# A 512-token transformer stack on one core: causal mask of the sparse attention taken from the matmuls into VectorE's maximum, norm factors spread in f32r, and a few side operations in other places

## The reference

```python
def rmsnorm(x, g): x * rsqrt(mean(x*x)) * g          # seven of them
h = rmsnorm(x, norm); proj = h @ w                   # 128-wide strips of w
# layer 0: y = conv3(u * b) * c  (three-tap causal convolution), plus memory attention
# layer 1: sliding window attention with sinks, plus memory attention
# both:    x = x + (silu(h @ w_gate) * (h @ w_up)) @ w_down
# second block, sparse attention: 4 query blocks of 128, 8 heads in 2 groups
s = einsum('qghd,qgnbd->qghnb', q, ks) * scale       # selected keys: with 512 tokens all of them
p_s = masked_softmax(s, kpos <= t)                   # causal
p_w = masked_softmax(q @ kw * scale, causal window)  # window 512: again causal over all
p_c = masked_softmax(q @ kc, cmp_end <= t)           # 31 compressed keys
o = g0 * (p_c @ vc) + g1 * (p_s @ vs) + g2 * (p_w @ vw)
# retention over 4 heads; out = x + rmsnorm(merged @ w_out)
```

## Time and profile before

| | us |
|---|---|
| median of 3 runs | 1632.66 (1632.55 to 1633.41) |
| the profiled execution, its own time | 1633.12 |
| span of its trace | 1631.0 |
| TensorE busy | 1618.7 (99%) |
| VectorE busy | 876.8 (54%) |
| ScalarE busy | 573.2 (35%) |
| GpSimd busy | 124.7 (8%) |
| granted TensorE clock | 0.999 |

### The profile page before, as it was taken

How to read it: one execution, slowest core, us unless ns; L and a number is a source line. 1 busy time by engine, 2 the same in 40 slices (tenths; PEclk the granted TensorE clock), 3 DMA queues, 4 the chain that set the end, 5 groups by cost and what they waited for, 6 DMA issues and landing times.

```text
span 1631.0 us, 20597 instructions
## 1 busy us (share of the span) xinstructions
PE 1618.7 (99%) x7722; PEld 1300.9 (80%) x7722; DVE 876.8 (54%) x1190; ACT 573.2 (35%) x973; POOL 124.7 (8%) x114
## 2 busy tenths in 40 slices
PE   9999999999999999999999999999999999999998
PEld 7977888888888876778888888887777678888887
DVE  7566644444523366764444443337576656556444
ACT  6333432223222345543232223322345542234222
POOL 2000200000000000030000001114111001000000
PEclk9999999999999999999999999999999999999999
DMA  6422332322332341132322232243111121232222
GB/s 217 142 78 80 102 98 90 103 92 101 115 106 89 72 109 46 39 111 90 103 90 99 94 121 90 99 169 118 52 65 52 40 71 39 84 104 91 94 101 90
DMA packets 44588, 152.74 MB, mean 94 GB/s; under 512 B 5515, under 2 KB 8812, under 8 KB 44012
## 3 DMA queue, kind: packets, MB, share of 16 engines
q1 hardware_dynamic: 43744, 149.22, 27.9%
q10 hardware_dynamic: 780, 2.65, 0.6%
HBM read 149.46 MB, written 2.39 MB: 93 GB/s over the span
## 4 chain that ended last, share of the span: by engine, by line
PE 96%; DVE 2%; issue 1%; ACT 1%; DMA 0%; POOL 0%; DVEq 0%; POOLq 0%; ACTq 0%
PE ps L1841 27%; PE ps L1843 27%; PE ps L1842 27%; PE ps L2218 1%; PE ps L2232 1%; PE ps L2254 1%; PE ps L2278 1%; PE ps L2334 1%; PE ps L2333 1%; PE ps L2332 1%; PE ps L2042 1%; DVE w_lo L1109 1%; PE ps L2060 1%; PE ps L2075 1%; PE ps L2268 1%
## 5 line engine op out<-in xcount | busy, mean ns | idle before, releaser
L1841 PE MATMUL ps<-a_hi,w_hi 128*128 128x512 f32 x1336 | 530.6, 397 | 1.9 <-DVE a_lo L1114 1.1
L1843 PE MATMUL ps<-a_hi,w_lo 128*128 128x512 f32 x1336 | 520.8, 390 | 0.0
L1842 PE MATMUL ps<-a_lo,w_hi 128*128 128x512 f32 x1336 | 520.4, 390 | 0.0
L1109 DVE TENSOR_TENSOR w_lo<-raw,w_hi 128x1024 fp32r<-128x1024 f32 (+4 forms) x257 | 331.2, 1289 | 247.1 <-ACT w_hi L704 241.9
L704 ACT ACTIVATE w_hi<-raw 128x1024 fp32r<-128x1024 f32 (+4 forms) x257 | 270.2, 1051 | 284.1 <-PE ps L1843 264.5
L1841 PEld LDWEIGHTS ps<-a_hi,w_hi 128*128 128x128 f32 x1336 | 250.9, 188 | 62.6 <-issue 9.1
L1843 PEld LDWEIGHTS ps<-a_hi,w_lo 128*128 128x128 f32 x1336 | 250.8, 188 | 53.1
L1842 PEld LDWEIGHTS ps<-a_lo,w_hi 128*128 128x128 f32 x1336 | 251.1, 188 | 50.3 <-issue 1.0
L1135 DVE TENSOR_TENSOR tmp<-ps,rstd 128x512 f32<-128x512 f32 x121 | 83.5, 691 | 185.8 <-PE ps L1843 175.6
L1841 PE MATMUL ps<-g_hi,w_hi 128*128 128x512 f32 x352 | 136.9, 389 | 0.0
L1842 PE MATMUL ps<-g_lo,w_hi 128*128 128x512 f32 x352 | 136.9, 389 | 0.0
(11 more groups left out here) (301 smaller groups left out, 1811.5 us busy)
## 6 DMA issues: line engine op xcount, KB each, us to landing
raw<-w SPq DMA_DIRECT2D x134, 512.0 KB, 3.4
raw<-w8b SPq DMA_DIRECT2D x70, 512.0 KB, 3.4
raw<-w_down SPq DMA_DIRECT2D x32, 704.0 KB, 4.0
w<-cmp_w SPq DMA_DIRECT2D x2, 2048.0 KB, 10.7
raw<-w_out_first SPq DMA_DIRECT2D x8, 320.0 KB, 2.8
raw<-w_nsa_o SPq DMA_DIRECT2D x8, 256.0 KB, 2.8
out<-o_t SPq DMA_DIRECT2D x8, 256.0 KB, 2.0
x<-xT SPq DMA_DIRECT2D x7, 256.0 KB, 6.7
```

The costliest lines, as they stand in the source:

```text
L1109: dve.tensor_tensor(w_lo[:, slot, 0:w], raw[:, raw_slot, 0:w], w_hi[:, slot, 0:w].bitcast(F32), ALU.subtract).then_inc(w_lo_ready, 1)
L1841: pe.matmul(o, wh, a_h, start=start and at == 0, stop=False)
L1842: pe.matmul(o, wh, a_l, start=False, stop=False)
L1843: ins = pe.matmul(o, wl, a_h, start=False, stop=stop and at == kt - 1)
```

## The change

1. **Mask.** The four mask matmuls of each unit go. VectorE's one reduce becomes four `tensor_tensor_reduce` (one for each head), which read the scores from PSUM and a bf16 table `ahead` [128, 512], write the masked, negated scores to `p_n` and the bias to `nmx`. ScalarE's exponential then reads `p_n` in SBUF. The score banks are free after the maximum (`ns_max`) and no longer after the exponential. `ahead` is a new load of SP, behind `cmp_pe`; `masks` shrinks.
2. **Spreads.** `rs` is split into `rs_hi` and `rs_lo` by two small VectorE operations, two diagonals are made, and `spread` is two f32r matmuls. `diag_lo` lies over `acc`, so that GpSimd's `clear` waits for the spread before it.
3. **Places.** `spread(V_MIX0)` goes from tile 3 to 5 of strip 3, `spread(V_MEM)` from the border into tile 3 of strip 9, `spread(V_MIX1)` from tile 1 to 3. Four of the memory's eight squares go one and two strips later. The convolution of tile 0 goes from n=4 to n=5, behind `split(6)`. In N_OUT2 the squares come three strips later, VectorE's `operand` one strip later, and `split(N_FFN1+1)` behind the last operands. `sw_turn(7, 0)`, `hidden` and `ns_turn(15, (2, 3))` go from a border into the strip behind it. `ns_maxima` comes ahead of the `split` in VectorE's queue, ScalarE's `ns_normalise(0)` ahead of the compressed exponential, and `cmp_normalise` is cut in two.

The core of the diff:

```diff
             def clear(v):
                 if v:
-                    pool.wait_ge(norm_sum, v)
+                    pool.wait_ge(norm_spread, v)
...
-                if n in (3, 4):
-                    for k in range(4 * n - 12, 4 * n - 8):
+                if n in (3, 4, 5):
+                    for k in ((0, 1, 2, 3), (4, 5), (6, 7))[n - 3]:
                         square(V_MEM, k, k % 2, memx[:, k, :], NMEM, first=k < 2)
...
-            out_phase(N_OUT2, V_FFN1, G_FFN1)
+            for m in range(KT):
+                split(N_OUT2 + m + 2, late_width(N_OUT2 + m + 2))
+                act.wait_ge(lin_read, out_index(N_OUT2 + m) + 1)
+                operand(m, G_FFN1)
+                if m >= 3:
+                    square(V_FFN1, m - 3, (m - 3) % 2, x[:, m - 3, :], first=m < 5)
+            for k in range(KT - 3, KT):
+                square(V_FFN1, k, k % 2, x[:, k, :], first=False)
...
             def ns_exps(u):
-                b, jp, br, keys = ns_unit(u)
-                act.wait_ge(ns_max, u + 1)
-                if u >= 2:
-                    act.wait_ge(ns_turned, GH * (u - 1))
+                keys = ns_unit(u)[3]
                 for j in range(GH):
-                    act.activation(p_n[:, u % 2, j, 0:keys], ps[:, 2 + j, 0:keys], ACT.Exp,
-                                   bias=nmx[:, u % 2, j:j + 1], accum_out=den[:, u % 2, j:j + 1])\
+                    act.wait_ge(ns_max, GH * u + j + 1)
+                    act.activation(p_n[:, u % 2, j, 0:keys], p_n[:, u % 2, j, 0:keys], ACT.Exp,
+                                   bias=nmx[:, u % 2, j:j + 1], scale=-1.0, accum_out=den[:, u % 2, j:j + 1])\
                         .then_inc(ns_exp, 1)
...
             def diagonal(v, tiles=TB, rs=rs):
 
                 dve.wait_ge(norm_pow, v + 1)
-                dve.tensor_tensor(diag[:, 0:tiles, :],
-                                  ident[:].unsqueeze(1).to_broadcast([P, tiles, P]),
-                                  rs[:, 0:tiles].unsqueeze(2).to_broadcast([P, tiles, P]), ALU.mult)\
-                    .then_inc(norm_diag, 1)
+                if v:
+                    dve.wait_ge(norm_spread, v)
+                dve.tensor_copy(rs_hi[:, 0:tiles], rs[:, 0:tiles]).then_inc(norm_part, 1)
+                dve.wait_ge(norm_part, 2 * v + 1)
+                dve.tensor_tensor(rs_lo[:, 0:tiles], rs[:, 0:tiles], rs_hi[:, 0:tiles].bitcast(F32), ALU.subtract)\
+                    .then_inc(norm_part, 1)
+                dve.wait_ge(norm_part, 2 * v + 2)
+                for part, diag in ((rs_hi, diag_hi), (rs_lo, diag_lo)):
+                    dve.tensor_tensor(diag[:, 0:tiles, :],
+                                      ident[:].unsqueeze(1).to_broadcast([P, tiles, P]),
+                                      part[:, 0:tiles].bitcast(F32).unsqueeze(2).to_broadcast([P, tiles, P]),
+                                      ALU.mult).then_inc(norm_diag, 1)
...
                 elif what == 1:
                     scaled(n, bank, v_s[:])
...
+                    if i:
+                        convolve(n, i)
...
                 if n in (3, 4, 5, 9):
                     split(n + 1, KT * P)
+                if n == 5:
+                    convolve(N_CONV0 + 1, 0)
...
             for m in range(KT):
                 residual(m, N_OUT2 + m, out_bank(N_OUT2 + m))
-                split(N_OUT2 + m + 2, late_width(N_OUT2 + m + 2))
-                if m > 1:
-                    operand(m - 2, G_FFN1, 3 * KT + m - 1)
-            for k in (KT - 2, KT - 1):
+                if m < KT - 1:
+                    split(N_OUT2 + m + 2, late_width(N_OUT2 + m + 2))
+                if m > 2:
+                    operand(m - 3, G_FFN1, 3 * KT + m - 2)
+            for k in range(KT - 3, KT):
                 operand(k, G_FFN1, 3 * KT + k + 1)
+            split(N_FFN1 + 1, late_width(N_FFN1 + 1))
...
             def ns_maxima(u):
...
-                dve.tensor_reduce(nmx[:, u % 2, :], ps[:, 2:6, 0:keys], AX.X, ALU.max, negate=True)\
-                    .then_inc(ns_max, 1)
...
+                for j in range(GH):
+                    dve.tensor_tensor_reduce(p_n[:, u % 2, j, 0:keys], ps[:, 2 + j, 0:keys],
+                                             ahead[:, S - keys:S], -1.0, FAR, ALU.add, ALU.min,
+                                             nmx[:, u % 2, j:j + 1]).then_inc(ns_max, 1)
...
+                if NS_FIRST < n < NS_FIRST + NS:
+                    ns_maxima(n - NS_FIRST)
+                if n == NS_FIRST + 1:
+                    cmp_weights()
                 if n + 1 == N_GATE:
                     gate_split()
...
             def spread(v, tiles=TB):
 
-                pe.wait_ge(norm_diag, v + 1)
-                pe.matmul(ps[:, stat_bank, 0:tiles * P], ones[:],
-                          diag[:, 0:tiles, :].rearrange("p b t -> p (b t)"),
-                          start=True, stop=True).then_inc(norm_spread, 1)
+                pe.wait_ge(ones_r_ready, 1)
+                for part, diag in enumerate((diag_hi, diag_lo)):
+                    pe.wait_ge(norm_diag, 2 * v + part + 1)
+                    ins = pe.matmul(ps[:, stat_bank, 0:tiles * P], ones_r[:],
+                                    diag[:, 0:tiles, :].rearrange("p b t -> p (b t)"),
+                                    start=part == 0, stop=part == 1)
+                ins.then_inc(norm_spread, 1)
...
-                if n == 3 and at == 3:
+                if n == 3 and at == 5:
                     spread(V_MIX0)
+                if n == 9 and at == 3:
+                    spread(V_MEM, 2)
...
-                for k in range(GH):
-                    ins = pe.matmul(ps[:, 2 + k, b * P:keys], ident_b, causal, start=False, stop=True)
                 ins.then_inc(ns_scores, 1)
...
+                if k == 0 and u == NS - 1:
+                    ns_turn(u, (2, 3))
                 if k == 0 and ns_unit(u)[2]:
                     cmp_turn(u)
```

More of the change, by code:

```diff
@@ L96 @@
 EMPTY = -1.0e29
+FAR = 3.0e38
 TINY = float(np.finfo(np.float32).tiny)
@@ L135, in build @@
     diag_at = main[0]
-    diag = sb(main, "diag", [P, TB, P])
+    diag_hi = sb(main, "diag_hi", [P, TB, P], R32)
+    acc_at = main[0]
     acc = sb(main, "acc", [P, S])
@@ L141, in build @@
     acc2 = sb(main, "acc2", [P, S])
-    main[0] += K1
+    ahead = sb(main, "ahead", [P, S], BF16)
+    ones_r = sb(main, "ones_r", [P, P], R32)
     w2 = sb(main, "w2", [P, 2, 2, HD])
     ident = sb(main, "ident", [P, P])
-    masks = sb(main, "masks", [P, 2 * P + TB * NCMP], BF16)
+    masks = sb(main, "masks", [P, P + TB * NCMP], BF16)
     vc = sb(main, "vc", [NCMP, 2, HD])
@@ L155, in build @@
     kc = sb(rest, "kc", [P, 2 * NCMP])
+    rs_hi = sb(rest, "rs_hi", [P, TB], R32)
+    rs_lo = sb(rest, "rs_lo", [P, TB], R32)
     rs2 = sb(rest, "rs2", [P, TB])
@@ L250, in build @@
     ident_b = masks[:, 0:P]
-    causal = masks[:, P:2 * P]
-    mask_c = masks[:, 2 * P:].rearrange("p (b c) -> p b c", b=TB)
+    mask_c = masks[:, P:].rearrange("p (b c) -> p b c", b=TB)
     ps = nc.alloc_psum_tensor("ps", [P, 8, S], F32)
@@ L280, in build @@
     norm_diag = sem("norm_diag")
+    norm_part = sem("norm_part")
+    ones_r_ready = sem("ones_r_ready")
     norm_spread = sem("norm_spread")
@@ L370, in build @@
     ns_scores = sem("ns_scores")
+    ahead_in = sem("ahead_in")
     ns_max = sem("ns_max")
@@ L542, in _ @@
             sp.dma_start(pe2[:], a["cmp_pe"]).then_inc(small2_in, 16)
+            sp.dma_start(ahead[:], a["ahead"]).then_inc(ahead_in, 16)
             with sp.Fori(1, N_DOWN0 // RAW, 1) as i:
@@ L630, in power @@
                     .then_inc(norm_pow, 1)
+            pool.wait_ge(ones_ready, 1)
+            pool.tensor_copy(ones_r[:], ones[:]).then_inc(ones_r_ready, 1)
             clear(V_MIX0)
@@ L1219, in conv_low, with convolve @@
                     .then_inc(yc_lo_ready, 1)
+            def convolve(n, i):
+                dve.wait_ge(lin_read, n + 1)
+                dve.tensor_tensor(v_s[:], v_s[:], u_s[:], ALU.mult).then_inc(conv_step, 1)
+                dve.wait_ge(conv_step, 5 * i + 1)
+                dve.tensor_scalar(y_s[:], v_s[:], conv_w[:, i, 2:3], None, ALU.mult).then_inc(conv_step, 1)
+                for back in (1, 2):
+                    dve.wait_ge(conv_step, 5 * i + 1 + back)
+                    dve.scalar_tensor_tensor(y_s[:, back:S], v_s[:, 0:S - back],
+                                             conv_w[:, i, 2 - back:3 - back], y_s[:, back:S],
+                                             ALU.mult, ALU.add).then_inc(conv_step, 1)
             def l0_epilogue(n):
@@ L1953, in _ @@
                     sums(V_MEM, 2)
-                if n == 9:
-                    spread(V_MEM, 2)
                 if N_MEMKV + 6 <= n <= N_MEMKV + 9:
@@ L1977, in _ @@
                     else:
-                        strip(n, mem_hi, mem_lo, bank_of(n), cols=NMEM)
+                        strip(n, mem_hi, mem_lo, bank_of(n), cols=NMEM, aside=lambda at, n=n: begin_beside(n, at))
```

(29 more changed lines are left out.)

25 lines of the change are left out of this document (15 added, 10 removed).

## The result

The changed kernel takes 1635.95 us (median of 20 runs, 1633.47 to 1636.55), the kernel before 1632.79 (20 runs, 1632.19 to 1633.58). The ratio is 1.0017, 95% interval 1.0011 to 1.0024: 0.17% slower, less than the 0.2% that counts as a difference here, where 1628.2 us and "faster" had been forecast. The profiled execution took 1634.9 us with a span of 1633.1, against 1633.12 and 1631.0 before.

What follows compares the result with a forecast made beforehand. TensorE bounds the kernel, holding 96% of the chain of waits. Savings of 8.5 us (3.7 + 2.3 + 2.5) less costs of 4.05 (0.45 + 2.8 + 0.8) net 4.4 us: 1628.2 us median, range 1624.2 to 1631.5.

Steps and rivals of the forecast that it cites:

- No rival: Four rivals: convolution costs nothing 12%, FFN1 starts without waits 11%, maximum at half rate 5%, change does less 20%.
- Masks: In the 16 units: dropping four mask matmuls saves 0.23 us each, 3.7 us; VectorE's added work is hidden.
- waits of units 0 and 1: TensorE's waits in the first two units: 1.3 us by starts, 0.6 stays, so 0.7 us less.
- Rival (c): In the units: the new maximum runs at half rate for its bf16 operand, 15 us more, 1643 us; chance 5%.
- Spreads: Norm-factor spreads: two f32r matmuls instead of one plain; five save 2.05 us, the memory's 0.25, sum 2.3 us.
- wait on the low diagonal ahead of strip 187: Ahead of strip 187: nothing covers VectorE's longer chain, 0.45 us given back (bounds 0.3 and 0.7).
- Waits that go: TensorE waits at the memory's diagonal, sliding-window turn, `hidden` and the first two units go: 2.5 us less.
- Diagonal, window, `hidden`: Three TensorE waits that go: memory's diagonal 0.6 us by starts, sliding-window turn 0.5, `hidden` on the windows 0.7.
- `ns_turn(15, (2, 3))`: In the last unit: its 0.5 us wait only changes its name, gain taken as 0 (bounds 0 and 0.5).
- The convolution: Short strips: tile 0's convolution behind `split(6)` makes strip 7 wait for `w_lo`, 2.8 us more (bounds 2.3 and 3.5).
- Start of FFN1: Ahead of FFN1's second strip: sums wait for four late GpSimd sums, 0 to 1.9 us later, taken as +0.8.
- The signs given: No L2221, spreads at half distance, waits on `w_lo`, `acc` and low diagonal, none on L1585 in units 2 to 15.

Runs made afterwards that it cites:

- both moves undone: Changed kernel with tile 0's convolution back in strip 3's epilogue and the last projection's squares, operands and splits in their old order: 1626.06 us.
- the 13 added matmuls: Changed kernel with matmuls nobody reads in TensorE's long waits, 9 ahead of strip 7 and 13 ahead of FFN1's sums: 1632.09 us.
- best: Changed kernel with convolution and last projection back in their old order, except the split for FFN1's second strip stays behind the last operands: 1625.61 us.
- squares or order: Changed kernel with the convolution and ScalarE's last-projection squares back in their old places, VectorE's new order kept: 1625.27 us.

## Why the prediction was wrong

The forecast was 1628.2 us, the median 1635.95: 7.75 us more, outside the range of 1624.2 to 1631.5, and of the other sign. No rival held the outcome either. The steps, in the order of the prediction:

**Masks: right.** No L2221; no wait on VectorE's normalisation but 0.2 us in one unit. About 2.7 us by the two traces (3.4 over all units, less the 0.7 of the waits of units 0 and 1), 3.4 by the runs, for 3.7. Rival (c) fell: the new maximum runs at full rate, 0.69 us at 512 columns, which is the 0.7 estimated.
```profile
L1609 DVE CUSTOM_DVE_ANT_0 p_n<-ps,ahead 128x512 f32<-128x512 f32 x16 | 10.1, 688 | 6.4 <-PE ps L2267 6.4
```

**Spreads: right.** Between the two traces each spread gained its 0.4 us. Two f32r matmuls, 0.45 us from the first to the next tile:
```profile
743.38 0.39 PE L1922 MATMUL ps<-diag_hi,ones_r 128*128 128x512 f32 x1
743.60 0.39 PE L1922 MATMUL ps<-diag_lo,ones_r 128*128 128x512 f32 x1
743.83 0.39 PE L1884 MATMUL ps<-a_hi,w_hi 128*128 128x512 f32 x1
...
1110.83 0.19 PEld L1922 LDWEIGHTS ps<-diag_lo,ones_r 128*128 128x128 f32 x1 [0.35 <-DVE diag_lo L1149]
```
The last row is the wait on the low diagonal ahead of strip 187, 0.35 us by the record for 0.45 forecast. By the runs they are worth 1.2 us for the 1.85 forecast, and the difference is in the short strips, where the start-up also moves TensorE by more than that.

**Waits that go: right.** Diagonal, window, `hidden` and units 0 and 1 gained about what was written; `ns_turn(15, (2, 3))` gained nothing, the wait only changed its name (L2289 on L997, 0.6 us). The kernel with both moves undone gains 6.8 us in all, where these three parts were 3.7 + 2.3 - 0.45 + 2.5 = 8.05. By its starts 3.4 us of the gain are there at unit 0's scores (1154.92 against 1158.28 us), for the 3.65 forecast up to that point, and 3.3 come in the units, for 4.4: most of the 1.25 us short is in the units.

**The convolution: right in its wait, and the wait was only two thirds of its price.** The list has 2.9 us, for 2.8 (bounds 2.3 and 3.5); by starts it is 3.0, of which 1.3 only take back TensorE's lead from the start-up. What failed is that I stopped at the wait. Behind it the clock was at 1.2 GHz for 3.4 us, 1.5 us more in the profiled execution.

**Start of FFN1: the term that was mis-sized.** I took +0.8 us and up to 1.9. TensorE went from 0.9 us behind to 4.1 at the sums, 3.2 net. Two steps failed. I took the four sums left at 1.38 each, 5.5 us; they took 7.07, as VectorE's four operands and its split ran in the same time:
```profile
725.43 0.67 DVE L1171 TENSOR_TENSOR x<-x,ps 128x512 f32<-128x512 f32 x1
726.03 3.76 DVE L1129 SCALAR_TENSOR_TENSOR a_lo<-x,gains,a_hi 128x512 fp32r<-128x512 f32 x4
...
727.47 7.07 POOL L631 TENSOR_TENSOR acc<-acc,sq 128x512 f32<-128x512 f32 x4 [2.51 <-ACT sq L724]
729.72 2.30 DVE L1124 TENSOR_TENSOR w_lo<-raw,w_hi 128x1024 fp32r<-128x1024 f32 x1
```
That is 1.55 us. My own rows had half of it: a sum beside VectorE was 1.58 in the earlier trace rows, four of them are 6.3 us, and I took 1.38, near the 1.30 of one alone. And they began 0.4 us later against TensorE than written. The rest of the miss is that I settled on 0.8 where my sum gave 1.2. Then came the clock, 2.4 us more by starts, which I had not priced at all.

**The clock: the missing term.** Filling both waits gives 4.35 us back, over half of the 7.75. The prediction has no term for the clock, and so counts it as 1.00 throughout; it never asked what waits of three to four times the longest in the trace (1.0 us) would do to it. By the Trainium skill (TensorE: Matmul & The Clock Gate, Part 1: The HAM clock gate) the lower level is the default and activity lifts it. The runs here agree: the same two places with TensorE busy in them, 1.00 and 4.35 us less. With that page in mind the slower outcome could have stood as a rival. No run here shows when a wait is followed by a fall: behind the same 2.9 us one profile has it and one has not.

Together, from the medians: 4.35 us for the clock; 1.9 for the two moves without it (5.5 for 2.8 + 0.8), by the traces the start of FFN1 alone is 2.4 too much (3.2 for 0.8), and the convolution's move comes out somewhat below its 2.8; and 1.25 for what the rest gained less (6.8 for 8.05). These are 7.5 of the 7.75 us.

**The signs given** were there, L2221 gone, spreads at half the distance, 2.9 us on `w_lo` at strip 7, `acc` named by TensorE (until 734.6 us, not 731), but for 0.2 us on VectorE's normalisation in one late unit. They would have told me that the mechanisms were right, and none of them asks how long the price runs on behind a wait.

## What to carry to other kernels

Price a new long wait of TensorE with the stretch behind it: here waits of 2.0 to 3.8 us were followed by 1.2 GHz for 3.4 us or more in all profiled executions but one, and matmuls that nobody needs, put into the wait, won that part back. When work is shifted later, count what is left of it behind the last operand on the slowest engine of its chain, at the rate that it has beside its neighbour then (GpSimd's sum is 1.3 us alone and up to 2.9 beside VectorE). Split a change into its parts before dropping it: two of its moves hid 6.8 us of gain in the others. Before a wait near the start is laid to an edit, compare where TensorE stood when it came there: the start-up alone moved it by up to 1.4 us between these profiles.

## What the runs showed that I had not expected

The clock can fall after the idle time, not in it: with the 13 added matmuls the wait of 0.9 us behind them and the one-column sums, 0.9 us by starts, were over at 734.0 us, TensorE then ran at 2.4 GHz to 735.3, and only there the clock fell, for 3.6 us (735.3 to 738.9). In `best`, a wait of 0.8 us and the same one-column sums (727.15 to 728.07) were followed by no fall.

GpSimd and VectorE don't share the time evenly, they take turns. A sum of 1.26 us took 1.43 to 1.78 us where it had to let one VectorE operation end, and 2.90 where two went ahead of it; a VectorE operand of 0.74 us took 1.77 beside a sum. The Trainium skill (SBUF — State Buffer, SBUF: two separate sides) has it that the one that starts first keeps the shared port for its whole instruction. The sum of 2.90 us at 724.20 in `best`, which ended 1.14 us after the split beside it (724.75 + 1.21), agrees in that the two exclude each other: VectorE's operations ran at their full speed in front of it. Who goes first is not settled by the recorded starts: this sum's record starts ahead of the split that passed it, while in the kernel of "squares or order" a sum at 724.12, with four VectorE operands in a row beside it, came in behind one of them and took 1.78. I had cited this rule in the prediction and not priced the sums by it.

What stays open is how the fall of the clock depends on the wait. Behind 0.9 us it came once (with the 13 added matmuls) and once not (both moves undone, strip 6), behind 0.8 us it did not (`best`); behind 2.0 and 2.2 us it came; behind 2.9 us it came in the changed kernel and did not in the one with the last projection in its old order.
